# Inverting the 64x64 triangular blocks of a gated delta rule: two doubling levels replaced by substitution in 8x8 blocks on VectorE

## What is computed

```python
a_mat = jnp.where(tri_strict, beta[..., None] * kk * decay, 0.0)      # 64 x 64 a chunk
eye = jnp.eye(c, dtype=jnp.float32)
rhs = jnp.concatenate([v * beta[..., None], k * (beta * jnp.exp(G))[..., None]], axis=-1)
sol = lax.linalg.triangular_solve(a_mat + eye, rhs, left_side=True, lower=True, unit_diagonal=True)
value, k_cum = sol[..., :dv], sol[..., dv:]
```

## Time and profile before

| | |
|---|---|
| median of three runs | 1999.79 us (1999.75 to 1999.91) |
| profiled execution | 2000.0 us |
| its span, first to last instruction | 1998.2 us |
| mean granted TensorE clock | 0.995 of full |
| TensorE busy | 1956.5 us (98%), 10421 matmuls |
| VectorE busy | 906.6 us (45%) |
| ScalarE (ACT) busy | 688.6 us (34%) |
| GpSimd busy | 931.8 us (47%) |

### The profile page before, as it was taken

How to read it: one execution, slowest core, us unless ns; L and a number is a source line. 1 busy time by engine, 2 the same in 40 slices (tenths; PEclk the granted TensorE clock), 3 DMA queues, 4 the chain that set the end, 5 groups by cost and what they waited for, 6 DMA issues and landing times.

```text
span 1998.2 us, 28267 instructions
## 1 busy us (share of the span) xinstructions
PE 1956.5 (98%) x10421; PEld 1599.6 (80%) x10421; DVE 906.6 (45%) x1567; ACT 688.6 (34%) x1383; POOL 931.8 (47%) x711
## 2 busy tenths in 40 slices
PE   7999999999999999999999999999999999999997
PEld 5787778777788888888888888888778888888886
DVE  4766776677652222121212366576532234234143
ACT  4333333433342223232324344544332233222122
POOL 3443344434434456445445633234244565546455
PEclk9999999999999999999999999999999999999998
DMA  5122202222223443333333322112132323323232
GB/s 191 54 85 73 72 27 79 84 63 59 67 64 95 124 155 93 106 96 95 95 94 96 125 85 74 52 63 67 60 137 92 108 83 97 106 85 105 90 102 74
DMA packets 52902, 178.50 MB, mean 89 GB/s; under 512 B 6688, under 2 KB 7520, under 8 KB 52576
## 3 DMA queue, kind: packets, MB, share of 16 engines
q1 hardware_dynamic: 52336, 174.88, 27.4%
q10 hardware_dynamic: 496, 2.65, 0.4%
HBM read 173.29 MB, written 4.23 MB: 89 GB/s over the span
## 4 chain that ended last, share of the span: by engine, by line
PE 93%; DVE 4%; issue 1%; ACT 1%; DMA 0%; POOL 0%; POOLq 0%; DVEq 0%; SPq 0%; ACTq 0%
PE bank L286 27%; PE bank L288 26%; PE bank L287 26%; PE bank L1527 2%; PE bank L1516 2%; PE bank L1510 2%; PE bank L986 1%; PE bank L1703 1%; PE bank L1690 1%; PE bank L970 1%; PE bank L956 1%; PE bank L930 0%; DVE raw_z L1905 0%; PE bank L1567 0%; DMA residual<-x_t 0%
## 5 line engine op out<-in xcount | busy, mean ns | idle before, releaser
L275 POOL TENSOR_TENSOR slab_lo<-slab_raw,slab_hi 128x512 fp32r<-128x512 f32 x604 | 824.8, 1391 | 967.5 <-ACT slab_hi L268 967.4
L286 PE MATMUL bank<-u_hi,slab_hi 128*128 128x512 f32 x1584 | 657.5, 415 | 17.4 <-POOL slab_lo L275 13.4
L288 PE MATMUL bank<-u_hi,slab_lo 128*128 128x512 f32 x1584 | 620.6, 392 | 0.0
L287 PE MATMUL bank<-u_lo,slab_hi 128*128 128x512 f32 x1584 | 619.1, 391 | 0.0
L268 ACT CAST slab_hi<-slab_raw 128x1024 fp32r<-128x1024 f32 x302 | 313.9, 1045 | 219.5 <-PE bank L288 218.4
L286 PEld LDWEIGHTS bank<-u_hi,slab_hi 128*128 128x128 f32 x1584 | 299.0, 189 | 79.6 <-issue 23.1
L288 PEld LDWEIGHTS bank<-u_hi,slab_lo 128*128 128x128 f32 x1584 | 298.0, 188 | 65.0
L287 PEld LDWEIGHTS bank<-u_lo,slab_hi 128*128 128x128 f32 x1584 | 299.5, 189 | 53.7 <-issue 1.9
L286 PE MATMUL bank<-hidden_hi,slab_hi 128*128 128x512 f32 x432 | 168.4, 390 | 0.3
L287 PE MATMUL bank<-hidden_lo,slab_hi 128*128 128x512 f32 x432 | 168.1, 389 | 0.0
L288 PE MATMUL bank<-hidden_hi,slab_lo 128*128 128x512 f32 x432 | 168.1, 389 | 0.0
(11 more groups left out here) (340 smaller groups left out, 2627.1 us busy)
## 6 DMA issues: line engine op xcount, KB each, us to landing
slab_raw<-slabs SPq DMA_DIRECT2D x302, 512.0 KB, 3.5
g_and_cum_rows<-row_store SPq DMA_DIRECT2D x7, 512.0 KB, 6.4
residual<-x_t SPq DMA_DIRECT2D x2, 1024.0 KB, 7.2
x_tok<-x SPq DMA_DIRECT2D x1, 2048.0 KB, 12.8
residual<-x_t SPq DMA_DIRECT2D x1, 2048.0 KB, 9.2
residual_store<-residual SPq DMA_DIRECT2D x1, 2048.0 KB, 9.8
residual<-residual_store ACTq DMA_DIRECT2D x1, 2048.0 KB, 9.0
out_t<-residual SPq DMA_DIRECT2D x8, 256.0 KB, 2.1
```

The costliest lines, as they stand in the source:

```text
L275: ins = pool.tensor_tensor(w_lo[s][:, ks, :], raw[s][:, ks, :], w_hi[s][:, ks, :].bitcast(F32), ALU.subtract)
L286: pe.matmul(bank, w_hi[s][:, k, :], x_hi[:, k, :], start=first, stop=False)
L287: pe.matmul(bank, w_hi[s][:, k, :], x_lo[:, k, :], start=False, stop=False)
L288: mm = pe.matmul(bank, w_lo[s][:, k, :], x_hi[:, k, :], start=False, stop=last)
```

## The change

Levels 0, 1 and 2 are replaced. GpSimd masks the diagonal 8x8 blocks of A (`bm`). VectorE gathers them to 8 columns a tile by a strided sum over the eight blocks of a row (`bx`, a reduction of 256 elements to 32) and multiplies that with a constant so that each row's 8 values stand in the columns of their own row index. One matmul with the constant `same_block` (128x128, ones in 8x8 diagonal blocks) spreads them, so that every partition holds all 64 values of its block (`bs`, 256 columns; ACT copies them into `lanes`). Each partition then holds one column of its block's inverse, and VectorE finds its 8 elements by substitution, two rows at a time (`bi`: a product, a sum and a copy, three pairs of product and reduction, an expansion back to 128x256, a transpose). Levels 3 to 6 go on as before. The tokens `z0`, `xt`, `Y1`, `X1`, `Y2`, `X2` go, `bm`, `bx`, `bs`, `bi` come, and other tokens of the list are moved: `Y3` comes at s1.4, `dm` and `qk` go from s1.0 to behind s2.3 and s2.5, the convolution taps `cv0.0` to `cv0.3` come later by three to five slab parts, `Y5` is ahead of `cv0.2` and `P3`, and `T3` behind s3.1 instead of behind s3.3. One more constant is loaded. GpSimd does four masks a head instead of six.

```diff
-        ORDER = """fvt s0.0 dif s0.1 colb fr bd s0.2 eg fk s0.3 kk th3 s0.4 S0 s0.5 z0 s0.6 xt sl3 E0 s0.7 dm qk s1.0 Y1
-                   e0 s1.1 tv P0 s1.2 vp s1.3 s1.4 X1 kpd T0 S1 s1.5 E1 s1.6 Y2 qd P1 s1.7 O0 s2.0 X2 e1 T1 S2 s2.1
-                   E2 cv0.0 s2.2 Y3 O1 s2.3 cv0.1 P2 X3 s2.4 cv0.2 s2.5 Y4 T2 s2.6 S3 cv0.3 s2.7 X4 E3 s3.0 e2 O2 s3.1 Y5
-                   th0 P3 s3.2 cv1.0 s3.3 X5 T3 cv1.1 s3.4 sl0 s3.5 Y6 O3 cv1.2 s3.6 tq s3.7 X6 cv1.3 s4.0 e3 s4.1 vk
+        ORDER = """fvt s0.0 dif s0.1 colb fr bd s0.2 eg fk s0.3 kk th3 s0.4 S0 s0.5 bm s0.6 bx E0 s0.7 P0 sl3 s1.0 bs
+                   s1.1 tv T0 bi s1.2 e0 s1.3 S1 s1.4 Y3 vp E1 s1.5 kpd s1.6 P1 s1.7 X3 s2.0 e1 O0 s2.1 T1 S2 s2.2
+                   Y4 E2 qd s2.3 O1 P2 dm s2.4 X4 s2.5 T2 qk S3 s2.6 cv0.0 E3 s2.7 cv0.1 O2 s3.0 Y5 cv0.2 P3 e2 s3.1
+                   T3 cv0.3 s3.2 X5 cv1.0 th0 s3.3 cv1.1 s3.4 sl0 s3.5 Y6 O3 cv1.2 s3.6 tq s3.7 X6 cv1.3 s4.0 e3 s4.1 vk
...
+                def blocks_spread():
+                    pe.wait_ge(sem("blk"), 2 * c + 2)
+                    pe.matmul(bA[:, 0:NT * B8 * B8], same_block[:], blk_rhs[:].rearrange("p a b -> p (a b)"),
+                              start=True, stop=True).then_inc(sem("blk_ps"), 1)
...
+                def blocks_spread():
+                    act.wait_ge(sem("blk_ps"), c + 1)
+                    act.copy(lanes[:, :, :, 0:2, 1:].rearrange("p n m r k -> p (n m) r k"),
+                             bA[:, 0:NT * B8 * B8].rearrange("p (m r k) -> p m r k", r=2, k=B8)).then_inc(sem("blk_rows"), 1)
...
+                def blocks_gather():
+                    dve.wait_ge(sem("blk_masked"), c + 1)
+                    dve.tensor_reduce(blk[:].rearrange("p (n i) -> p n i", n=NT),
+                                      atm[0].rearrange("p (n b i) -> p n i b", n=NT, i=B8), AX.X, ALU.add)\
+                        .then_inc(sem("blk"), 1)
+                    dve.wait_ge(sem("blk"), 2 * c + 1)
+                    dve.tensor_tensor(blk_rhs[:], blk[:].unsqueeze(2).to_broadcast([P, NT * B8, B8]),
+                                      level_mask[:, 1, 0:B8].unsqueeze(1).to_broadcast([P, NT * B8, B8]), ALU.mult)\
+                        .then_inc(sem("blk"), 1)
+
+                def blocks_inverse():
+
+                    dve.wait_ge(sem("blk_rows"), c + 1)
+                    factor = lanes[:].rearrange("p n m r k -> p n (m r k)")[:, :, 2 + B8:12 * (1 + B8):3 * (1 + B8) + 2]
+                    step(dve.tensor_tensor(lane_prod[:], lanes[:, :, :, 0, :],
+                                           factor.unsqueeze(3).to_broadcast([P, NT, B8 // 2, 1 + B8]), ALU.mult))
+                    step(dve.tensor_tensor(lanes[:, :, :, 2, :], lanes[:, :, :, 1, :], lane_prod[:], ALU.add))
+                    step(dve.tensor_copy(lane_x[:, :, 1:3], lanes[:, :, 0, 0:3:2, 0]))
+                    for m in range(1, B8 // 2):
+                        w = 2 * m + 1
+                        step(dve.tensor_tensor(lane_prod[:, :, 0:2, 0:w], lanes[:, :, m, 0:3:2, 0:w],
+                                               lane_x[:, :, 0:w].unsqueeze(2).to_broadcast([P, NT, 2, w]), ALU.mult))
+                        step(dve.tensor_reduce(lane_x[:, :, w:w + 2], lane_prod[:, :, 0:2, 0:w], AX.X, ALU.add))
+                    dve.tensor_tensor(zi[:].rearrange("p (n b i) -> p n b i", n=NT, i=B8),
+                                      lane_x[:, :, 1:].unsqueeze(2).to_broadcast([P, NT, HB // B8, B8]),
+                                      half_tiles(level_mask[:, 2, :]).rearrange("p n (b i) -> p n b i", i=B8), ALU.mult)\
+                        .then_inc(sem("z_new"), 1)
+                    dve.wait_ge(sem("z_new"), 5 * c + 1)
+                    dve.transpose(xi, zi[:]).then_inc(sem("x_new"), 1)
...
                 def level(l):
-                    if l == 0:
-                        pool.wait_ge(sem("masked"), c + 1)
-                    elif l == 2:
-                        pool.wait_ge(sem("z0"), c + 1)
-                    elif l > 2:
-                        pool.wait_ge(sem("y_ps"), 6 * c + l - 2)
+                    if l == L8 + 1:
+                        pool.wait_ge(sem("blk"), 2 * c + 1)
+                    elif l > L8 + 1:
+                        pool.wait_ge(sem("y_ps"), 4 * c + l - L8 - 1)
                     pool.tensor_tensor(c4(atm[l % 2]), c4(a_c), half_tiles(level_mask[:, l, :]), ALU.mult)\
                         .then_inc(sem("atm"), 1)
+
+                def blocks_mask():
+                    pool.wait_ge(sem("masked"), c + 1)
+                    pool.tensor_tensor(c4(atm[0]), c4(a_c), half_tiles(level_mask[:, 0, :]), ALU.mult)\
+                        .then_inc(sem("blk_masked"), 1)
+                    level(L8)
...
+                stages = {"nsq": lambda: norm_pool_scale(pool, 0), "cola": cols_, "osq": osq, "bm": blocks_mask, "bi": lambda: level(L8 + 1)}
+                stages[f"Y{L8 + 1}"] = lambda: level(L8 + 2)
```

More of the change, by code:

```diff
@@ L34 @@
 LEVELS = 7
+B8, L8 = 8, 3
 HB, QB = 64, 32
@@ L38 @@
 SLOTS = 4
-DVE_STEPS, LATE_STEPS = 26, 10
+DVE_STEPS, LATE_STEPS = 35, 10
 LEAD = 2
@@ L302, in program @@
         neg_mask = head("neg_mask", [P, P])
+        same_block = head("same_block", [P, P])
         h_small = head("h_small", [P, NQ, NT])
@@ L323, in program @@
         zi, zf = head("inv_t", [P, HW]), head("inv_t_full", [P, T])
+        blk, blk_rhs = head("blocks", [P, NT * B8]), head("blocks_spread", [P, NT * B8, B8])
+        lanes = head("block_rows", [P, NT, B8 // 2, 3, 1 + B8])
+        lane_prod = head("block_products", [P, NT, B8 // 2, 1 + B8])
+        lane_x = head("block_inverse", [P, NT, 1 + B8])
         th = [bdt, adt, bdt, adt]
@@ L1619, in qk @@
                     tiles(bB, ck, cq).then_inc(sem("qk_ps"), 1)
+                def blocks_spread():
+                    pe.wait_ge(sem("blk"), 2 * c + 2)
+                    pe.matmul(bA[:, 0:NT * B8 * B8], same_block[:], blk_rhs[:].rearrange("p a b -> p (a b)"),
+                              start=True, stop=True).then_inc(sem("blk_ps"), 1)
                 def level_y(l):
                     if l < LEVELS - 1:
[L1623 to L1627, removed]
+                        pe.wait_ge(sem("atm"), 3 * c + l - L8 + 1)
+                    pe.wait_ge(sem("x_new"), 4 * c + l - L8 + 1)
                     if l < LEVELS - 1:
@@ L1637, in level_x @@
                 def level_x(l):
-                    pe.wait_ge(sem("y"), 6 * c + l)
-                    if l == 1:
+                    pe.wait_ge(sem("y"), 4 * c + l - L8 + 1)
+                    if l == L8:
                         pe.wait_ge(sem("v_rhs"), c + 1)
-                    if l > 1:
-                        pe.wait_ge(sem("z_new"), 6 * c + l - 1)
+                    else:
+                        pe.wait_ge(sem("z_new"), 5 * c + l - L8 + 1)
                     if l < LEVELS - 1:
@@ L1652, in vk @@
                 def vk():
-                    pe.wait_ge(sem("z_new"), 6 * c + 6)
+                    pe.wait_ge(sem("z_new"), 5 * c + 5)
                     pe.wait_ge(sem("setup_dve"), 1)
@@ L1709, in head_round @@
                           "gates3": gates3, "fr": fr,
-                          "fvt": fvt_, "tv": tv, "kk": kk, "qk": qk, "vk": vk, "ot": ot}
+                          "fvt": fvt_, "tv": tv, "kk": kk, "qk": qk, "vk": vk, "ot": ot, "bs": blocks_spread}
                 for x, tok in enumerate(("tq", "tfq", "tk", "tfk")):
                     stages[tok] = lambda x=x: square_t(x)
-                for l in range(1, LEVELS):
+                for l in range(L8, LEVELS):
                     stages[f"Y{l}"] = lambda l=l: level_y(l)
@@ L2132, in head_round @@
                           "gates1": gates1, "gates2": gates2, "cola": cola, "colb": colb, "colh": colh, "dif": dif,
-                          "bd": bd, "dm": dm, "qd": qd, "fk": fk, "kpd": kpd, "vp": vp_, "kk": kk, "qk": qk, "z0": z0,
-                          "xt": xt, "vk": vk, "osq": osq, "on": on_, "oa": oa}
+                          "bd": bd, "dm": dm, "qd": qd, "fk": fk, "kpd": kpd, "vp": vp_, "kk": kk, "qk": qk,
+                          "bx": blocks_gather, "bi": blocks_inverse, "vk": vk, "osq": osq, "on": on_, "oa": oa}
                 for k in range(KT):
@@ L2217, in constants @@
     r, c = np.arange(P)[:, None], np.arange(P)[None, :]
-    masks = [((c // b) % 2 == 1) & ((r // b) % 2 == 0) & (r // (2 * b) == c // (2 * b))
-             for b in (2 ** l for l in range(LEVELS - 1))] + [r == c]
+    block = r // B8 == c // B8
+    masks = [block & (c > r), -1.0 * (c == r % B8), block]
+    masks += [((c // b) % 2 == 1) & ((r // b) % 2 == 0) & (r // (2 * b) == c // (2 * b))
+              for b in (2 ** l for l in range(L8, LEVELS - 1))] + [c == r % B8]
     f = np.float32
```

30 lines of the change are left out of this document (12 added, 18 removed).

## The result

| | before | after |
|---|---|---|
| median | 1999.85 us (4 runs) | 2010.42 us (4 runs, 2009.81 to 2011.53) |
| profiled execution, span | 1998.2 us | 2007.9 us |
| matmuls | 10421 | 9925 |
| TensorE busy | 1956.5 us | 1942.5 us |

The ratio is 1.0052, with a 95% interval of 1.004 to 1.0064: slower, though 14 us of matmul time are gone. The chain that ended last shows what took its place. TensorE's share has fallen from 93 to 91%, VectorE's has risen from 4 to 6%, and "issue" from 1 to 2%.

What follows compares the result with a forecast made beforehand. TensorE was taken to bound the kernel. Inner rounds -2.63 + 0.05 + 2.6 + 1.5 = +1.5 us, x7 = +10.6, last round -0.7, first +0.2: together +10, giving 2009.5 us, range 1997 to 2016.

Steps and rivals of the forecast that it cites:

- TensorE's saving: Levels 1 and 2 dropped, spread matmul added, old waits gone: TensorE alone 2.63 us a round less, if nobody is late.
- The hold of the substitution by GpSimd: GpSimd's split and level 4 mask hold product, sum and copy in inner rounds, so Y3 waits 2.6 us.
- rival with small instructions unheld: Substitution beside the split of s1.0 isn't held: waits 0.1 and 0.65, -1.8 us a round, about 1986 us; chance 0.15.
- Prices: New VectorE work costs 0.16 us + 1.04 ns an element and 0.04 us a gap; substitution 3.3 us if unheld.
- rival of a lower fixed cost: VectorE instructions have a lower fixed cost than the profile rows show: about 2003 us; chance 0.05.
- the gather: VectorE's reduction over 256 elements ahead of the spread takes 0.43 us; the spread then waits 0.05 us.
- T3: The fourth tile's probabilities come late behind the taps and a GpSimd split, so TensorE waits 1.5 us at T3.
- rival with P3 ahead of the split: P3 gets its turn before the split, leaving only one wait: +0.65 us a round, 2003.5 us; chance 0.15.
- Inner rounds: Saving and waits at the spread, Y3 and T3 sum to +1.5 us a round, +10.6 us over seven.
- The last round and the first: Last head round -0.7 us, with no T3 wait but a 2.5 us wait at Y3; first round +0.2 us.

Runs made afterwards that it cites:

- e8: Convolution tap cv0.3 moved from ahead of X5 to behind it, on top of e3; 1980.55 us, ratio 0.99.
- e2: Kernel after the change with GpSimd's split of the slab at s1.0 moved behind the substitution's transpose in inner rounds; 1990.99 us, ratio 0.9954.
- e6: Kernel after the change with only GpSimd's level 4 mask moved behind the substitution's transpose, the split left beside it; 2005.10 us, ratio 1.0023.
- e7: Kernel after the change without the substitution's three pairs of product and reduction, so the output isn't the reference's; 1993.29 us, ratio 0.9965.
- e9: On top of e4, bi alone moved from the place of X1 to behind P1; 2014.24 us, ratio 1.0065.
- e3: Kernel after the change with the edits of e1 and e2 together; 1982.56 us, ratio 0.9909.
- e1: Kernel after the change with only T3 moved, from behind s3.1 back to behind X5; 1998.86 us, ratio 0.9994.
- e5: On top of e2, P3 put ahead of cv0.2 and T3 left where the change put it; 1984.86 us, ratio 0.9923.
- e4: Kernel after the change in the old order, substitution tokens at the places of z0, xt, Y1 and X1; 2007.26 us, ratio 1.0035.

## Why the prediction came out right, and where its terms were off

2009.5 us were forecast and 2010.42 measured. The waits and what causes them are as forecast. That the total agrees within 1 us is luck: against the forecast's terms the inner rounds came out 2.9 us lower and the first and last round together 2.1 us lower, and falls of the clock, which had no term, added 4.6 us.

- **TensorE's saving.** Forecast 2.63 us a round. After the change an inner round without a fall of the clock, less the counted waits (2.15 + 1.23 + 0.25), is 65.80 - 3.63 = 62.17, and e8, which has removed the two large ones, measured 62.2. So the saving is 2.5 us; the term was 0.1 too large.
- **The hold of the substitution by GpSimd.** Right in mechanism and size: e2 removes all of Y3's wait by moving one split, e6 frees one instruction with one mask, e7 shows the rest of the chain unheld. The product, sum and copy were the three that I named. Y3 was forecast at 2.6 us of wait and had 2.2 (2.15 by the view). The rival with small instructions unheld is refuted. The Trainium skill, SBUF: State Buffer, Who interferes with whom, makes no exception for small instructions; the trace agrees, with 0.59 us for 8 elements in this kernel and 1.14 in e9.
- **Prices.** 144 elements 0.31 us, 24 to 56 elements 0.18 to 0.22, expansion 0.42, transpose 0.45, all as forecast from rows of other shapes, broadcast or strided. The Trainium skill, VectorE: DVE Perf Modes, gives in its table for the TRN2 errata 58 cycles + 1 an element, 0.21 us for the 144 elements. The measured 0.31 (in e3) decides against that row. But the prediction read the row alone: the text right below the table says that it is too low, and gives (N + 151) / 0.96 ns for an f32 tensor_tensor, measured at 512 and 2048 elements. For 144 elements that is 0.31 us, an estimate by that page, and the trace agrees. The rival of a lower fixed cost falls with it. Its 2003 us had been counted as slower, though it lies within the 4 us that the forecast calls no change. Only the gather was off: 0.66 us (0.62 to 0.67 in all kernels) against 0.43, which made the spread wait 0.25 us and not 0.05.
- **T3.** Forecast 1.5 us, measured 1.4 (1.23 by the view). The place, the taps ahead of P3 and the hold by the split at 436.72 are as forecast; e1 and e5 remove it in two ways. The rival with P3 ahead of the split is refuted by its 1.18 us.
- **Inner rounds** thus came to +1.10 us against the +1.5 summed: 7.7 us instead of 10.6.
- **The clock** has no term in the forecast, which says that a wait put in costs its length. Three falls of 1.53 us add 4.6 us beyond the waits' lengths. This is the step that the forecast lacked.
- **The last round and the first.** Forecast -0.7 and +0.2; measured -2.0 and -0.6 by the starts of the rounds. In the last round I had taken Y3's wait of the inner rounds (2.5 us), with the split of s1.0 beside the substitution. In that round's list s1.0 stands behind `bi`, and the split begins at 547.26, so nine of the instructions ran free and only the expansion was held. Y3 waited 0.95 us there and X3 0.53. VectorE there, product, sum, expansion:

```profile
545.15 0.31 DVE L2083 TENSOR_TENSOR block_products<-block_rows 128x144 f32<-128x144 f32 x1
545.50 0.31 DVE L2085 TENSOR_TENSOR block_rows<-block_rows,block_products 128x144 f32<-128x144 f32 x1
...
547.44 1.38 DVE L2092 TENSOR_TENSOR inv_t<-block_inverse,level_mask 128x256 f32<-128x256 f32 x1
```

Sum: -0.6 + 7.7 + 4.6 - 2.0 = 9.7 us, which is the difference of the spans.

What stays open is which waits let the clock fall. By kernel, with the longest wait of an inner round and the falls in seven rounds: e3, e5 and e8 0.5 us or less, none; e7 0.8 at Y3 and 1.2 at T3, none; e2 1.2, none; e6 1.8, two; e1 2.2, one; after 2.2, three; e9 2.7, six. In e4 every inner round has a wait of 1.5 us at O0 and one of 1.2 at T1, 2.4 us from start to start, and the clock fell in one of the seven. So a wait of 1.5 us or more is in every round that fell, but behind equal waits the clock fell in one round and not in the next, and what decides between them isn't shown. In the last round of e4, behind a wait of 3.4 us, the clock was at the lower level for some 7 us (0.50 from 546 to 552).

## What to carry to other kernels

TensorE bounds this kernel, and moving work from it to VectorE saved what it took only where the chain of small dependent instructions was placed by two conditions at once: nothing that is wanted early stands behind it in VectorE's queue (e4), and no GpSimd work runs beside it (e2, e9). One GpSimd instruction of 1.3 us held a copy of 8 elements, which needs 0.17 us, to 1.14 (e9); moving that split by four slab parts turned +0.5% into -0.5%, and with two more tokens of the order moved (T3 and cv0.3) into -1%. When a wait of two us is put into TensorE's stream, look at its clock behind it as well.

## What the runs showed that I had not expected

- In a TensorE stream that is otherwise nearly without a break the granted clock fell to its lower level, 1.2 GHz, shortly behind waits of 1.5 to 2.7 us, in some rounds and not in others (in every second one in the kernel after the change). In that kernel it lasted about 3.5 us. A fall cost 1.5 us there, in e1 and in e6, and 1.25 us in e4.
- A reduction of 256 elements to 32 with a stride of 8 elements took 0.62 to 0.67 us, where one of 256 to 1 takes 0.42. Whether stride or number of results costs it wasn't measured apart. A GpSimd mask ran beside it each time (from 410.08 to 410.87 in the round shown), so a hold isn't excluded either; against it, the reduction of 128 elements beside the same mask (at 410.30) took 0.29 us, which is the 0.42 of 256 elements less 128 elements at 1.04 ns each.
